# A hybrid encoder layer on one core: decay buffers by turn, and new orders for the block-product phase

## The reference

```python
def token_mixer(h, ...):
    proj = h @ w_in                       # z, xbc, dt, q, k, v, gates
    xs, Bm, Cm = split(silu(depthwise_conv(xbc)))
    y = ssd_scan forward + ssd_scan backward + xs * d_skip      # 16 heads of 64
    br_ssm = rmsnorm(y * silu(z), g_ssm) @ w_br_ssm
    br_attn = blocked_attention(rope(rmsnorm(q)), rope(rmsnorm(k)), v) @ w_br_attn   # 8 heads, 2 kv heads
    g_s, g_a = split(sigmoid(gates))
    return (g_s * br_ssm + g_a * br_attn) @ w_out

x = x + token_mixer(rmsnorm(x, g_mix))
x = x + moe_ffn(rmsnorm(x, g_ffn))        # top 4 of 32 experts, each 1024 -> 2048 -> 1024
return rmsnorm(x, g_final)
```

## Time and profile before

| | |
|---|---|
| median of 3 runs | 1243.3 us (1242.6 to 1246.64) |
| the profiled execution | 1242.42 us |
| its span | 1240.6 us |
| PE busy | 1175.2 us (95%) |
| DVE busy | 395.1 us (32%) |
| ACT busy | 238.2 us (19%) |
| data moved by DMA | 448.99 MB, mean 362 GB/s |
| mean granted TensorE clock | 0.988 |

### The profile page before, as it was taken

How to read it: one execution, slowest core, us unless ns; L and a number is a source line. 1 busy time by engine, 2 the same in 40 slices (tenths; PEclk the granted TensorE clock), 3 DMA queues, 4 the chain that set the end, 5 groups by cost and what they waited for, 6 DMA issues and landing times.

```text
span 1240.6 us, 14746 instructions
## 1 busy us (share of the span) xinstructions
PE 1175.2 (95%) x5503; PEld 553.8 (45%) x5503; DVE 395.1 (32%) x1004; ACT 238.2 (19%) x542; POOL 22.0 (2%) x36
## 2 busy tenths in 40 slices
PE   8999787899999999999999999999999999999996
PEld 7888565788533333333333333333333333333332
DVE  4547566672323222222322222222222222222212
ACT  2224655401111111111111111111111111111112
POOL 0001100100000000000000000000000000000000
PEclk9999899899999999999999999999999999999999
DMA  9545442259999999999999999999999999999995
GB/s 309 181 136 176 144 140 85 69 186 426 411 428 428 427 428 426 428 428 427 428 427 428 428 428 428 428 429 428 428 431 427 427 430 427 429 428 427 428 427 230
DMA packets 71480, 448.99 MB, mean 362 GB/s; under 512 B 6536, under 2 KB 44044, under 8 KB 45837
## 3 DMA queue, kind: packets, MB, share of 16 engines
q1 hardware_dynamic: 68186, 446.85, 87.6%
q10 hardware_dynamic: 3251, 1.54, 0.5%
HBM read 447.29 MB, written 1.08 MB: 361 GB/s over the span
## 4 chain that ended last, share of the span: by engine, by line
PE 71%; DMA 19%; ACT 4%; DVE 3%; issue 1%; ACTq 0%; POOL 0%; SPq 0%; DVEq 0%
PE bank L976 40%; DMA ring<-in_w_mlp_dram 19%; PE bank L650 9%; PE bank L603 5%; PE bank L971 4%; PE bank L951 4%; PE bank L1015 1%; PE bank L960 1%; ACT arena L1515 1%; PE bank L834 1%; ACT arena L1334 1%; ACT arena L1324 1%; DVE arena L1835 1%; PE bank L965 1%; PE bank L884 1%
## 5 line engine op out<-in xcount | busy, mean ns | idle before, releaser
L976 PE MATMUL bank<-ring,arena 128*64 128x512 f32 x2928 | 654.9, 595 | 21.2 <-DMA ring<-in_w_mlp_dram 20.6
L976 PEld LDWEIGHTS bank<-ring,arena 128*64 128x64 f32 x2928 | 201.9, 137 | 418.4 <-issue 371.2
L2113 DVE TENSOR_TENSOR arena<-bank,b1T 128x256 f32<-128x256 f32 x126 | 53.0, 421 | 469.0 <-PE bank L1015 466.6
L1512 ACT ACTIVATE arena<-bank 128x512 f32<-128x512 f32 x32 | 19.1, 597 | 407.3 <-PE bank L976 407.3
L2099 DVE TENSOR_TENSOR arena<-bank,prmT 128x512 f32<-128x512 f32 x30 | 20.7, 692 | 181.4 <-PE bank L960 181.4
L971 PE MATMUL bank<-arena 64*128 64x512 f32 x256 | 63.6, 615 | 0.8 <-ACT arena L1562 0.8
L603 PE MATMUL bank<-hT,ring 128*128 128x256 f32 x288 | 63.0, 380 | 0.0
L951 PE MATMUL bank<-xres,arena 128*64 128x512 f32 x248 | 60.0, 604 | 0.0
L603 PEld LDWEIGHTS bank<-hT,ring 128*128 128x128 f32 x288 | 54.5, 190 | 7.7 <-issue 0.4
L650 PE MATMUL bank<-ring,spare 128*128 128x256 f32 x176 | 45.1, 402 | 11.0 <-DVE over L1755 11.0
L650 PE MATMUL bank<-spare 128*128 128x256 f32 x176 | 41.2, 384 | 7.3 <-ACT spare L1273 7.2
(11 more groups left out here) (283 smaller groups left out, 925.8 us busy)
## 6 DMA issues: line engine op xcount, KB each, us to landing
ring<-in_w_mlp_dram SPq DMA_DIRECT2D x184, 2048.0 KB, 30.8
ring<-in_w_in_dram SPq DMA_DIRECT2D x24, 1024.0 KB, 6.8
ring<-in_w_mlp_dram SPq DMA_DIRECT2D x10, 1024.0 KB, 29.8
ring<-in_w_br_attn_dram SPq DMA_DIRECT2D x4, 1024.0 KB, 5.1
ring<-in_w_br_ssm_dram SPq DMA_DIRECT2D x4, 1024.0 KB, 6.0
ring<-in_w_out_dram SPq DMA_DIRECT2D x4, 1024.0 KB, 6.4
arena<-in_w_mlp_dram SPq DMA_DIRECT2D x3, 1024.0 KB, 14.9
arena<-acs_rows SPq DMA_DIRECT2D x4, 512.0 KB, 5.7
```

What stands on the lines that cost most here:

```text
L976: return nc.tensor.matmul(bank[b][side * CAP:(side + 1) * CAP, :], tokens, w, start=start, stop=stop, skip_group_check=True)
L1512: nc.scalar.activation(hs[:, 0:512].rearrange("q (i p) -> q i p", i=4), bank[up][:, :].rearrange("q (p i) -> q i p", i=4), ACT.Copy).then_ ...
L2113: step(V.tensor_tensor(o, side(bank[up + b][:, :]), bias_h.to_broadcast([P, 4, CAP]), ALU.add))
```

## The change

The two buffers of decays. The weights are now made in place where the exponentials end, in one of two buffers of 1536 columns by turn; the third buffer is gone, and `decay_rows(g)` waits for the scan two turns back instead of the weights of the turn before:

```diff
-        decay = arena[:, 4880:5904].rearrange("p (h i l) -> p h i l", h=2, i=TT)
-        decay_all = arena[:, 4880:6416]
-        decay_diag = arena[:, 5904:6416].rearrange("p (h i l) -> p h i l", h=2, i=TT)
-        gbuf = arena[:, 6416:8464].rearrange("p (b h i l) -> p b h i l", b=2, h=2, i=TT)
+        decay_all = [arena[:, 4880 + 1536 * b:6416 + 1536 * b] for b in range(2)]
+        gbuf = [a[:, 0:1024].rearrange("p (h i l) -> p h i l", h=2, i=TT) for a in decay_all]
+        gdiag = [a[:, 1024:1536].rearrange("p (h i l) -> p h i l", h=2, i=TT) for a in decay_all]
...
-                    if g >= 1:
-                        act.wait_ge(g_ready, g)
+                    if g >= 2:
+                        act.wait_ge(y_psum, g - 1)
...
-                if g >= 2:
-                    dve.wait_ge(y_psum, g - 1)
                 dve.wait_ge(seg_exp, g + 1)
...
-                V.tensor_tensor(o, decay, cb[:, k, :, :].unsqueeze(1).to_broadcast([P, 2, TT, 256]), ALU.mult)
+                V.tensor_tensor(o, o, cb[:, k, :, :].unsqueeze(1).to_broadcast([P, 2, TT, 256]), ALU.mult)
```

SP's loads. The rows of sums are loaded between single unit loads, and six expert loads move ahead, in between the loads of the last eight units (`AWAY_EARLY` loses 88, which is loaded by itself):

```diff
+                if n == U_BS + 1:
+                    sp.wait_ge(o_psum, AH)
+                    load_away(88)
+                if n == U_BS + 3:
+                    sp.wait_ge(y_psum, KD)
+                    for u in AWAY_EARLY:
+                        load_away(u)
+                if n == U_O + 1:
+                    first_free(pair_at(0, True))
+                    load_first(0)
...
-            sp.wait_ge(y_psum, KD)
-            sp.wait_ge(o_psum, AH)
-            for u in AWAY_EARLY:
-                load_away(u)
-            for g in range(PAIRS - 1):
+            for g in range(1, PAIRS - 1):
```

The orders. `heads(g)` is taken apart into `prob_transposes(h)`, `head_values(h)` and `scan(g)`, `y_square(g)` into itself and `y_gain(g)`, `gated` into `quarter` and `merge`, and all three engines' lists from the key pair to the scan branch are written anew, one line of them for each function:

```diff
-            heads(0)
-            pair_steps(P_G, 5, 5)
...
+            prob_transposes(3)
+            scan(1)
+            pair_steps(P_G + 2, 3, 4)
+            head_values(3)
+            scores(5)
```

More of the change, by code:

```diff
@@ L753, in _ @@
             pair_steps(P_KV, 2, 7)
[L755 to L761, removed]
@@ L762, in _ @@
-            nc.tensor.matmul(sums[:, 1, 0, :], ones, dta[:, 1, b_], start=False, stop=True, skip_group_check=True).then_inc(acs_psum, 1)
-            pair_steps(P_Q, 1, 3)
[L764 to L768, removed]
+            pair_steps(P_Q, 1, 3)
+            decay_sums()
+            pair_steps(P_Q, 4, 6)
@@ L800, in _ @@
+            prob_transposes(7)
+            pair_steps(P_G + 3, 7, 7)
+            head_values(7)
+            scan(5)
             pe.wait_ge(o_ready, 7)
@@ L1406, in _ @@
             decay_rows(1, 0)
             decay_rows(1, 1)
+            score_exps(1)
+            qT_copy(3)
+            probT_copy(0)
+            decays(0)
+            first_part(P_G + 1)
             decays(1)
+            score_exps(2)
+            second_part(P_G + 1)
+            probT_copy(1)
             o_copy(0)
-            head_norm(4)
-            score_exps(1)
-            third_part(P_G)
-            qT_copy(2)
-            y_square(0)
+            gate(0)
+            qT_copy(4)
@@ L1444, in _ @@
-            p = P_G + 3
-            score_exps(6)
-            first_part(p)
-            gate(2)
+            o_copy(2)
+            gate(1)
+            first_part(P_G + 2)
+            y_square(0)
+            y_gain(0)
+            score_exps(4)
+            probT_copy(3)
+            decay_rows(3, 0)
+            decay_rows(3, 1)
+            second_part(P_G + 2)
+            decays(3)
+            o_copy(3)
+            y_square(1)
+            decay_rows(4, 0)
+            decay_rows(4, 1)
@@ new lines, in _ @@
+            probT_copy(4)
+            score_exps(5)
+            third_part(P_G + 2)
+            o_copy(4)
+            decays(4)
+            decay_rows(5, 0)
+            decay_rows(5, 1)
+            y_square(2)
+            first_part(P_G + 3)
+            decays(5)
+            probT_copy(5)
+            gate(2)
+            score_exps(6)
+            second_part(P_G + 3)
+            o_copy(5)
+            y_square(3)
+            decay_rows(6, 0)
+            decay_rows(6, 1)
+            score_exps(7)
@@ L1448, in _ @@
+            probT_copy(6)
+            third_part(P_G + 3)
+            decays(6)
+            y_gain(1)
+            y_square(4)
+            o_copy(6)
+            probT_copy(7)
+            y_gain(2)
+            y_gain(3)
+            y_gain(4)
+            o_copy(7)
+            decay_rows(7, 0)
+            decay_rows(7, 1)
+            first_part(P_BA)
             y_square(5)
-            decay_rows(7, 0)
-            second_part(p)
-            probT_copy(6)
-            decay_rows(7, 1)
+            y_gain(5)
@@ new lines, in _ @@
+            score_max(1)
+            quarter(P_G, 2)
+            quarter(P_G, 3)
+            weight_sum(P_G + 2, 2)
+            weight_sum(P_G + 2, 3)
+            quarter(P_G, 4)
+            prob_norm(1)
+            rope(4)
+            score_max(2)
+            decay_weights(0)
+            decay_weights(1)
+            prob_norm(2)
+            weight_sum(P_G + 2, 4)
+            score_max(3)
+            weight_sum(P_G + 3, 1)
+            quarter(P_G + 1, 1)
+            y_out(0)
+            prob_norm(3)
```

637 lines of the change are left out of this document (348 added, 289 removed).

## The result

The changed kernel takes 1204.05 us (median of four executions, 1203.58 to 1205.91); the kernel before, beside it, 1243.53. The ratio is 0.9685, 95% interval [0.9672, 0.9698]: 39.5 us or 3.15% faster.

The account below looks back on a forecast made before the run. PE's mixer work, which sets when the expert-weight stream begins, was taken as the bound: 1242.4 - 36.5 + 1.0 - 3.3 = 1203.6 us profiled, median 0.9 above, 1204.5. Own range 1200 to 1208; with rivals 1 (at its middle) and 2, 1199 to 1213.

Parts of the forecast that it names:

- The waits and slow matmuls, 36.5 us: Mixer's block products, middle stretch: 107.9 us against 71.4 at full clock, so PE loses 36.5 us, all expected to go.
- 1 us for thin margins: PE's block products: 1 us lost where waits end only 0.1 to 0.4 us before PE comes to them.
- middle stretch: Block products from first gate pair's fourth step, heads and scans woven in: 107.9 us before, about 72 expected at clock 1.00.
- one chain through all engines: A head's turn in the middle stretch: ACT, DVE and PE one after the other, 13.9 us a head.
- the orders walked side by side: Three engine orders walked with measured durations: no PE waits after the change; 24.5 us before, where rows say 24.7.
- 24.7 us of waits and 11.8 of slow matmuls: Middle stretch: nine PE waits of 24.7 us plus 11.8 us of slow matmuls after them make the 36.5 us loss.
- The stream's lead, 3.3 us: Expert-weight stream after the mixer: six loads issued earlier bring the end 3.3 us forward, bounded by 0 and 5.
- the cap: First pair for a used slot waits for PE; landing after issue can shorten only from 10.8 to 7.5 us.
- the stream at 428 GB/s without a break after the first used slot: Sign of being right: expert weights load at full rate once the first slot used by an expert is reloaded.
- Rival 1: Block products: DVE becomes the bound; a fifth slower, it leaves 9 us of PE waits, 1213.5 us; chance 0.17.
- Rival 3: Middle stretch: the clock falls all the same, keeping 11.8 us of slow matmuls, 1216.3 us; chance 0.03.
- Rivals 2, 4 and 5: 2: stream's lead whole, 9 us, 1198.8, 0.05; 4: stream alone sets end, 1243, 0.02; 5: SP held by waits, 1247, 0.03.

Follow-up runs that it names:

- filler run: The kernel before, with useless matmuls put into eight of PE's waits, 16.8 us in all: 1237.26 us, ratio 0.9952.
- the two runs with the loads alone: Changed kernel with six early expert loads put back behind the mixer's last unit load: 1204.92 us; kernel before with only those loads moved ahead: 1241.97 us, ratio 0.9988.
- the change with halved loads: The changed kernel, with the next four pairs for used slots also loaded in two 1 MB halves: 1203.14 us, ratio 0.9676.

## Why the prediction was right

It gave 1204.5 us and the range 1199 to 1213; the median is 1204.05. Step by step:

**The waits and slow matmuls, 36.5 us: right in size.** The phase went from 190.2 to 153.4 us, 36.8 less. The forecast for it, with the 1 us for thin margins, was 35.5 less, 154.7 us. Two small errors stand in the sum. It counts eight heads' scores in the middle stretch of before, where seven stand (the first one's come ahead of it, at 125.52 us), so the length at full clock was 70.4 us and the loss 37.5. And the margins took 0.4 us. As a sign of being right the prediction gave a middle stretch of "about 72 us"; between the same points it is 68.28 us, at clock 1.00, with DVE busy for 90% of it. The 72 had left in it the two scans that the prediction itself moves out (2.04 us), the transposes of a query pair that moved ahead (0.44) and the score counted too many (0.96): 71.4 - 3.4 + 0.4 of waits = 68.4.

**Why they go: shown as a whole, half wrong in its parts.** The text said that the maximum ahead of the decay weights, the four or five steps on PE between scores and transposes, and the freed decays break one chain through all engines. Two of these reasons fail alone: the swap of the maximum and the exponentials makes the kernel before slower by 0.62%, the freed buffers change nothing. Taken out of the changed kernel, the swap costs 2.4 us, and scores put close to the transposes cost 9.3. These are prices of single moves in the changed kernel and not shares of the 37 us: the scores stand closer there than before for two heads, and the swap has the other sign without PE's new order. Which of the moves (distances on PE, the scan and values set apart, the weight sums up to two pairs ahead, the last scans in the attention branch) brings how much wasn't tried and stays open. What holds as a whole is what the prediction used for the number: the orders walked side by side.

**24.7 us of waits and 11.8 of slow matmuls as a sum: right here, not in general.** The sum is the difference to a full-clock stretch and so holds once no wait is left. The filler run shows that the second part can't be had by itself: 7.4 us of it removed made the stretch 3.2 us shorter.

**1 us for thin margins: right in kind.** One wait of 0.36 us is left, on a quarter, at the end of the first gate pair and not in the second or third, where the closest margins were named.

**The stream's lead, 3.3 us: right for one landing, too large for the end.** The pair of the earlier trace rows lands 3.0 us sooner after its issue (7.8 against 10.8 us), as the cap had it. It is not the first load for a used slot, as the prediction took it to be: two halves of 1 MB stand ahead of it, and they land 5.1 us sooner (5.8 against 10.9). But the end gains about 1.5 us by the two runs with the loads alone (1.4 by the medians of the first, 1.5 by the ratio of the second, with 0.2 to 2.7 by its interval): inside the bounds of 0 to 5, and less than the 3.3 booked. The step that failed is "the stream at 428 GB/s without a break after the first used slot": the frees of the slots behind it hang on PE in the same way, and the stream stays under full rate in places until 328 us (217 GB/s at 300). The queue that was in front of the first one had filled those too.

**Rival 1, DVE as the bound** (1213.5): not so, but near. Its price was too small: it books 9 us of waits for a DVE slower by a fifth and no slow matmuls behind them. With 17.5 us more on DVE, less than a fifth of its 128, PE waits 8.7 us and the kernel takes 1216.6, 13 us more.

**Rival 3, the clock falls all the same** (1216.3): refuted. The granted clock is 1.00 over all 153.4 us, with eight transposes in a row from 137.81 to 138.84 us and a wait of 0.36 us directly behind them. The rule of the Trainium skill (TensorE: Matmul & The Clock Gate, Part 4) that transposes don't count as activity for the clock is not contradicted by this, since no run here holds a long stretch of transposes alone in the block products; no effect of it is seen in a phase where they are so few.

**Rivals 2, 4 and 5**: the lead did not come whole; PE's gain reached the end; SP's issues up to 252 us hold up no product, as PE waits for no load in this phase.

So the closeness of 1204.05 to 1204.5 is in part luck. For the profiled execution 1203.6 us were forecast and 1205.91 measured: the phase gave 1.3 us more than booked, what follows it 2.1 less (1.2 against 3.3), and the slow first matmuls cost 1.5. The median came out right because the profiled execution is 1.9 us over it, where the text had it 0.9 under.

## What to carry to other kernels

When several engines take turns on one item, look for the distance between its stages on the bounding engine first: in this kernel a swap on the helper engines was worth 2 us where the bounding engine had other work to do meanwhile, and cost 8 us without it. Before crediting a moved stage, walk all engines' hand-written orders with measured durations; here that gave a single wait's length and nearly its place (1.8 us forecast, 1.7 measured) where a reading of one engine's order gave the wrong sign. A load that is moved ahead gains only as far as the next loads' buffers come free sooner: count every wait for a used slot behind it, not only the first. And when stretches of two traces are compared, set both ends by the same instructions and not by the same microseconds.

## What the runs showed of the hardware

- In the block products the clock fell only behind waits of PE, but the length of a wait alone doesn't decide. Behind the waits of 2.56 and 2.45 us in the filler run the granted clock was down to 0.50 for a time (eight passes in 3.49 us instead of 1.89; four transposes in 1.12 us instead of 0.60). In the change with scores close, a wait of 1.21 us had no slow step behind it; neither had one of 2.70 us in the kernel before, at 189.08, nor one of 3.28 us in the run with the early loads alone:

```profile
174.73 1.99 PE L656 MATMUL bank<-ring,spare 128*128 128x256 f32 x8 [3.28 <-DVE over L1761]
```

- The first 16 matmuls of the first weight unit (32 passes) take 7.14 us in eleven of the thirteen profiles and 8.83 in two, all with the same program part; in the long ones the granted clock is 0.61 in the first 4.4 us. PE in order of time, the change and then the change with halved loads:

```profile
10.61 8.83 PE L586 MATMUL bank<-hT,ring 128*128 128x256 f32 x32 [0.73 <-DVE hT L1738]
```

```profile
9.95 7.14 PE L597 MATMUL bank<-hT,ring 128*128 128x256 f32 x32 [0.73 <-DVE hT L1749]
```

  Both profiled executions of the change had the longer one, and these were its slowest (1205.91 and 1206.28 us, mean clock 0.996; its seven others 1202.72 to 1205.51, at 0.997 to 0.999). What decides it is open; it is worth 1.7 us, about as much as the moved loads, so profiles are compared here by stage and not by span.
- 2 MB landed 7.8 us after their issue on a queue that had almost run empty, close to the 7.5 that the prediction worked out from a 1 MB load plus 1 MB at full rate.
